# Two-layer hybrid attention kernel: joined head sums, shifted slots in heads and layer 1, another order at the passages to the out stages

## The reference

```python
for layer in range(2):
    shift, scale, gate = split(silu(c) @ ada_w[layer] + ada_b[layer], 3)
    h = rms_norm(x, norm_w[layer]) * (1 + scale) + shift
    y = even_mixer(h) if layer == 0 else odd_mixer(h)
    x = x + gate * y
return rms_norm(x, final_norm_w)
# even_mixer, 8 heads: q, k, v, z = h @ w_in
#   differential attention: (softmax(q0 k0) - lam * softmax(q1 k1)) @ v, rms_norm over 128, * silu(z)
#   gated delta rule: q, k = l2_normalize(silu(conv(.))); chunks of 64, triangular solve,
#   scan over the state, rms_norm over 128, * silu(z);      then @ w_out
# odd_mixer, 32 heads in 4 groups: sliding window attention (128) with sinks, * silu(z), @ w_out
```

## Time and profile before

| | us |
|---|---|
| median of three runs (2013.40 to 2019.76) | 2015.92 |
| the profiled execution | 2020.77 |
| its span, first to last instruction | 2019.0 |
| TensorE busy, 12628 matmul instructions | 1906.0 (94%) |
| DVE, ACT busy | 1140.4, 735.1 |
| start of one head's values to the next's | 121.2 |
[...]

### The profile page before, as it was taken

How to read it: one execution, slowest core, us unless ns; L and a number is a source line. 1 busy time by engine, 2 the same in 40 slices (tenths; PEclk the granted TensorE clock), 3 DMA queues, 4 the chain that set the end, 5 groups by cost and what they waited for, 6 DMA issues and landing times.

```text
span 2019.0 us, 30586 instructions
## 1 busy us (share of the span) xinstructions
PE 1906.0 (94%) x12628; PEld 1471.2 (73%) x12628; DVE 1140.4 (56%) x2147; ACT 735.1 (36%) x1548; POOL 6.4 (0%) x9
## 2 busy tenths in 40 slices
PE   6899999999999999999998799899999999998996
PEld 0367778777777877778776688777777777776885
DVE  2365665656656466655755656745665565563333
ACT  3352342424334242342524322634443443343221
POOL 0000000000000000000000000000000000000001
PEclk8999999999999999999998899999999999998998
DMA  9942322232322322322220777433223232313333
GB/s 393 408 162 101 119 101 95 102 118 94 127 94 95 126 84 107 121 97 95 109 101 1 261 241 234 149 131 125 99 94 131 96 114 109 126 53 110 120 114 115
DMA packets 58314, 266.29 MB, mean 132 GB/s; under 512 B 6465, under 2 KB 6849, under 8 KB 40641
## 3 DMA queue, kind: packets, MB, share of 16 engines
q1 hardware_dynamic: 58176, 264.35, 35.8%
HBM read 255.41 MB, written 8.91 MB: 131 GB/s over the span
## 4 chain that ended last, share of the span: by engine, by line
PE 77%; DVE 10%; ACT 6%; DMA 4%; issue 2%; SPq 0%; DVEq 0%; ACTq 0%
PE psum L554 22%; PE psum L555 20%; PE psum L556 20%; DMA ada_p<-in_ada_first 2%; PE psum L657 2%; PE psum L944 2%; ACT pr L1315 2%; DVE ada_acc L1403 1%; PE psum L956 1%; PE psum L972 1%; PE psum L799 1%; DVE pr L1822 1%; DVE pr L1838 1%; PE psum L567 1%; DVE pa L1666 1%
## 5 line engine op out<-in xcount | busy, mean ns | idle before, releaser
L554 PE MATMUL psum<-mov_hi,w_hi 128*128 128x512 f32 x2128 | 875.9, 412 | 35.3 <-DVE mov_lo L1738 11.3
L555 PE MATMUL psum<-mov_lo,w_hi 128*128 128x512 f32 x2128 | 837.4, 394 | 0.0
L556 PE MATMUL psum<-mov_hi,w_lo 128*128 128x512 f32 x2128 | 836.7, 393 | 0.0
L554 PEld LDWEIGHTS psum<-mov_hi,w_hi 128*128 128x128 f32 x2128 | 403.3, 190 | 156.5 <-issue 63.5
L556 PEld LDWEIGHTS psum<-mov_hi,w_lo 128*128 128x128 f32 x2128 | 403.6, 190 | 89.0
L1388 DVE TENSOR_TENSOR w_lo<-w_raw,w_hi 128x512 fp32r<-128x512 f32 x532 | 356.2, 686 | 195.3 <-ACT w_hi L1042 194.7
L555 PEld LDWEIGHTS psum<-mov_lo,w_hi 128*128 128x128 f32 x2128 | 404.4, 190 | 77.7 <-issue 3.8
L1042 ACT ACTIVATE w_hi<-w_raw 128x512 fp32r<-128x512 f32 x532 | 309.2, 621 | 1.9 <-DMA w_raw<-in_w_pack 1.4
L1403 DVE SCALAR_TENSOR_TENSOR ada_acc<-ada_t,silu_c,ada_acc 128x512 f32<-128x512 f32 x240 | 179.2, 747 | 5.7
L1315 ACT ACTIVATE pr<-pr,st 128x256 f32<-128x256 f32 x128 | 63.4, 498 | 114.6 <-DVE st L1831 114.6
L1272 ACT ACTIVATE osq<-res 128x512 f32<-128x512 f32 x30 | 19.0, 632 | 235.2 <-DVE res L1777 235.2
(11 more groups left out here) (279 smaller groups left out, 1621.9 us busy)
## 6 DMA issues: line engine op xcount, KB each, us to landing
w_raw<-in_w_pack SPq DMA_DIRECT2D x133, 1024.0 KB, 4.8
ada_t<-in_ada_late SPq DMA_DIRECT2D x128, 512.0 KB, 5.7
x_in<-in_ada_first SPq DMA_DIRECT2D x32, 512.0 KB, 9.3
ada_t<-in_ada_first SPq DMA_DIRECT2D x16, 512.0 KB, 9.1
ada_p<-in_ada_first SPq DMA_DIRECT2D x16, 512.0 KB, 9.6
res<-in_x_t SPq DMA_DIRECT2D x4, 1024.0 KB, 11.3
xr<-in_x_t SPq DMA_DIRECT2D x16, 256.0 KB, 3.7
x_spill<-res SPq DMA_DIRECT2D x16, 256.0 KB, 5.4
```

The source lines that it names most:

```text
L554: mm(PJ[r], w_hi[r][:, ks], mov_hi[:, kt], start=(j == 0), stop=False)
L555: mm(PJ[r], w_hi[r][:, ks], mov_lo[:, kt], start=False, stop=False)
L556: ins = mm(PJ[r], w_lo[r][:, ks], mov_hi[:, kt], start=False, stop=(j == KC - 1))
```

## The change

- Heads: combine(3) stands in DVE's slot 15 instead of 17 (DA_C).
- Heads: the four sums become four matmuls with 32 output columns each, placed side by side in TensorE's columns, into four 32-row bands of one bank (all_sums, slot 21). ACT takes one Ln and one Exp over all 128 rows, with a bias for each band, behind a preload of the table that has both. all_spread (slot 23) brings each band's row back to 128 rows by four matmuls with 32 input rows each. DVE reads two of the results in PSUM, ACT copies the other two (spread_copies).
- Out stage 0: the first two pairs of adaLN tiles are issued ahead of the wait for dy_ok.
- Layer 1: scores and what follows one slot later, second turns at 20, values at 25 (71 for w = 3), adaLN tiles in slots 2, 4, 5, 6 of each 16 instead of 1, 5, 9, 13, ada_stage in slot 59 instead of 64, v_group in 14 instead of 12.
- Passage to out stage 1: the first blocks of y are split in the last group's slots 62 and 63 (half_ok tells when TensorE has read those of mov_hi that they replace); turns in slots 65 and 66, values in 68; the first out chunk runs two slots ahead of the second (TAIL1), splits in the order SPLIT1.

```diff
...
     c["slope1"] = np.broadcast_to(2.0 ** (-8.0 * np.arange(1, 33) / 32), (P, 32))
+    c["part"] = np.broadcast_to(np.repeat([1.0, 1.0 / P], 32), (P, 64))
+    c["spread"] = np.broadcast_to(p[:, None] % 32 == 0, (P, P))
+    c["nbias"] = np.stack([np.repeat([4 * EPS, 4 * EPS, EPS, 0.0], 32), np.repeat([0.0, -0.5 * np.log(P), 0.0, 0.0], 32)], axis=1)
...
-        DA_S, DA_T = (0, 5, 8, 13), (5, 8, 13, 18)
+        DA_S, DA_C, DA_T = (0, 5, 8, 13), (4, 7, 12, 15), (5, 8, 13, 18)
...
+        L1_T = [[(16 * w + 17, 16 * w + 20) for w in range(4)] for g in range(NG1)]
+        L1_V = [[16 * w + 25 for w in range(3)] + [71] for g in range(NG1)]
+        L1_T[-1][3], L1_V[-1][3] = (65, 66), 68
+        TAIL1 = [((0, 0), (0, 1))] + [((1, n), (0, n + 2)) for n in range(5)] + [((1, 5),), ((1, 6),)]
+        SPLIT1 = [range(4, 8), range(8, 10), range(10, 12), range(12, 15), range(15, 16)]
+        L1_ADA = (2, 4, 5, 6)
...
-                    if not base:
+                    if not base and n > 0:
                         ada_pair(8 * B_OUT0 + 2 * n)
                         ada_pair(8 * B_OUT0 + 2 * n + 1)
...
             load_w(0, 2, N_OUT0 + 1)
+            for n in range(2):
+                ada_pair(8 * B_OUT0 + n)
             sp.wait_ge(dy_ok, NH0)
...
+                if done is not None:
+                    ins.then_inc(done, 1)
...
-            def norm_sums(h, i):
-                pe.wait_ge(sqn_ok, h * 2 + i + 1)
-                if i == 0:
-                    mm(SA0, ones, tmpK[:], start=True, stop=True).then_inc(ssn_ok, 1)
-                else:
-                    mm(SA1, ones, tmpQ[:], start=True, stop=True).then_inc(ssn_ok, 1)
+            def all_sums(before, h):
+
+                if h is not None:
+                    pe.wait_ge(sqn_ok, h * 2 + 2)
+                if before is not None:
+                    pe.wait_ge(gsq_ok, before + 1)
+                    pe.wait_ge(dsq_ok, before + 1)
+                for q, buf in enumerate((tmpK, tmpQ, tA, pa[1])):
+                    if (h, before)[q // 2] is not None:
+                        ins = mm(SA0[Q[q], :], con("part")[:, 32 * (q // 2):32 * (q // 2) + 32], buf[:], start=True, stop=True,
+                                 tile_position=(0, 32 * q))
+                ins.then_inc(sums_ok, 1)
+
+            def all_spread(before, h):
+
+                pe.wait_ge(rn_ok, (before + 1 if h is None else h) + 1)
+                if before is not None:
+                    pe.wait_ge(ATev_ok, before * 4 + 4)
+                    pe.wait_ge(vn_ok, before * 4 + 4)
+                for q, out in enumerate((SA0, SA1, TR, GW)):
+                    if (h, before)[q // 2] is not None:
+                        ins = mm(out, con("spread", Q[q]), tmpK[Q[q], :], start=True, stop=True, tile_position=(32 * q, 0))
+                ins.then_inc(spread_ok, 1)
 
             def g_rows(h):
 
...
+                st[21] = [lambda: all_sums(before, h)]
+                st[23] = [lambda: all_spread(before, h)]
...
-                    st.setdefault(16 * w + 8, []).append(lambda w=w: scores1(g, w, 0))
-                    st.setdefault(16 * w + 10, []).append(lambda w=w: scores1(g, w, 1))
-                    st.setdefault(16 * w + 16, []).append(lambda w=w: turn1(g, 2 * w))
-                    st.setdefault(16 * w + 19, []).append(lambda w=w: turn1(g, 2 * w + 1))
-                    st.setdefault(16 * w + 22, []).append(lambda w=w: values1(g, w))
-                st[64].append(lambda: ada_stage(B_L1 + g, GW))
+                    st.setdefault(L1_T[g][w][0], []).append(lambda w=w: turn1(g, 2 * w))
+                    st.setdefault(L1_T[g][w][1], []).append(lambda w=w: turn1(g, 2 * w + 1))
+                    st.setdefault(L1_V[g][w], []).append(lambda w=w: values1(g, w))
+                    st.setdefault(16 * w + 9, []).append(lambda w=w: scores1(g, w, 0))
+                    st.setdefault(16 * w + 11, []).append(lambda w=w: scores1(g, w, 1))
+                st[59].append(lambda: ada_stage(B_L1 + g, GW))
...
+                    proj_slot(N_L1 + c, 8, g, s % SLOTS, free, done=half_ok if g == NG1 - 1 and s == 8 * SLOTS - 5 else None)
...
-                for c in range(2 if s < SLOTS - 1 else 0):
-                    proj_slot(N_OUT1 + c, 0, 0, s, ((q1_ok, z1_ok)[c], 4 * NG1), first=3 * KC)
+                for c, part in TAIL1[s]:
+                    proj_slot(N_OUT1 + c, 0, 0, part, ((q1_ok, z1_ok)[c], 4 * NG1), first=3 * KC)
...
             def all_rstd(before, h):
 
-
-
-                if before is not None:
-                    act.wait_ge(gss_ok, before + 1)
-                    step(f(tA[:], TR, ACT.Ln, scale=1.0 / P, bias=EPS))
-                    act.wait_ge(dss_ok, before + 1)
-                    step(f(pa[1][:], GW, ACT.Ln, scale=1.0 / P, bias=small[:, LEPS:LEPS + 1]))
-                if h is not None:
-                    for i, (dst, src) in enumerate(((tmpK, SA0), (tmpQ, SA1))):
-                        act.wait_ge(ssn_ok, h * 2 + i + 1)
-                        step(f(dst[:], src, ACT.Ln, bias=4 * EPS))
-                    for i, dst in enumerate((tmpK, tmpQ)):
-                        f(dst[:], dst[:], ACT.Exp, scale=-0.5, bias=(0.0, -0.5 * float(np.log(P)))[i]).then_inc(rn_ok, 1)
-                if before is not None:
-                    f(pa[1][:], pa[1][:], ACT.Exp, scale=-0.5).then_inc(drn_ok, 1)
-                    f(tA[:], tA[:], ACT.Exp, scale=-0.5).then_inc(grn_ok, 1)
+                rows = slice(0 if h is not None else 64, P if before is not None else 64)
+                nc.scalar.preload_act_table_set("natural_log_exp_and_others")
+                act.wait_ge(sums_ok, (before + 1 if h is None else h) + 1)
+                step(f(tmpK[rows, :], SA0[rows, :], ACT.Ln, bias=small[rows, NBIAS:NBIAS + 1]))
+                f(tmpK[rows, :], tmpK[rows, :], ACT.Exp, scale=-0.5, bias=con("nbias", rows)[:, 1:2]).then_inc(rn_ok, 1)
+
+            def spread_copies(before, idx):
+
+                act.wait_ge(spread_ok, idx + 1)
+                f(pa[1][:], GW, ACT.Copy).then_inc(drn_ok, 1)
+                f(tA[:], TR, ACT.Copy).then_inc(grn_ok, 1)
 
             def tail_stages(h):
...
                 st = head_stages(h)
...
-                    st.setdefault(16 * w + 16, []).append(lambda w=w: turn1_copy(g, 2 * w))
-                    st.setdefault(16 * w + 19, []).append(lambda w=w: turn1_copy(g, 2 * w + 1))
+                    st.setdefault(16 * w + 12, []).append(lambda w=w: exps1(g, 2 * w))
+                    st.setdefault(16 * w + 14, []).append(lambda w=w: exps1(g, 2 * w + 1))
+                    st.setdefault(L1_T[g][w][0], []).append(lambda w=w: turn1_copy(g, 2 * w))
+                    st.setdefault(L1_T[g][w][1], []).append(lambda w=w: turn1_copy(g, 2 * w + 1))
                 return st
 
...
                         h()
                     if s % 2 == 0:
                         split_hi(N_L1 + s // SLOTS + 1, 8, g, s % SLOTS // 2)
+                if g == NG1 - 1:
+                    split_y1(range(2, 4))
                 z1_tanh(g, 3)
+
+            def split_y1(ks):
+
+                for k in ks:
+                    act.wait_ge(y1_ok, k + 1)
+                    f(mov_hi[:, k * T:k * T + T], res[:, k * T:k * T + T], ACT.Copy).then_inc(hi_ok, 1)
 
             group(0)
             for g in range(1, NG1):
                 group(g, g - 1)
             tail = merged({}, group_stages(NG1 - 1))
-            for s in range(SLOTS):
+            for s in range(len(SPLIT1)):
                 for h in tail.get(s, []):
                     h()
-                for k in (2 * s, 2 * s + 1):
-                    act.wait_ge(y1_ok, k + 1)
-                    f(mov_hi[:, k * T:k * T + T], res[:, k * T:k * T + T], ACT.Copy).then_inc(hi_ok, 1)
-                if s < 4:
-                    split_hi(N_OUT1 + 1, 0, 0, s)
+                split_y1(SPLIT1[s][:2])
+                for q in ((0, 1), (2,), (3,), (), ())[s]:
+                    split_hi(N_OUT1 + 1, 0, 0, q)
+                split_y1(SPLIT1[s][2:])
 
             def final_scale(i, c):
...
                 V.tensor_copy(tile4(gB[:]), head_col(gate_g, h).to_broadcast([P, 4, P])).then_inc(gB_ok, 1)
 
             def norm_mul(h):
-                for i, (dst, n) in enumerate(((ck, tmpK), (cq, tmpQ))):
-                    dve.wait_ge(rn_ok, h * 2 + i + 1)
-                    V.tensor_tensor(dst[:], dst[:], n[:], ALU.mult).then_inc(qkn_ok, 1)
+                dve.wait_ge(spread_ok, h + 1)
+                for dst, n in ((ck, SA0), (cq, SA1)):
+                    V.tensor_tensor(dst[:], dst[:], n, ALU.mult).then_inc(qkn_ok, 1)
 
             def decay_exponents(h):
 
...
-                    st.setdefault(DA_T[b] - 1, []).append(lambda b=b: combine(h, b))
+                    st.setdefault(DA_C[b], []).append(lambda b=b: combine(h, b))
                 st.setdefault(24, []).append(lambda: gated(h, GO, tA, WDN, NH0, grn_ok, gy_ok))
...
             def group_stages(g):
```

(43 more changed lines are left out.)

36 lines of the change are left out of this document (16 added, 20 removed).

## The result

| | before | after |
|---|---|---|
| median (lowest to highest) of four runs, us | 2015.68 (2013.40 to 2019.76) | 1962.41 (1960.63 to 1966.31) |
| profiled execution, us | 2020.77 | 1966.31 |
| its span, us | 2019.0 | 1964.5 |
| mean granted TensorE clock | 0.979 | 0.981 |

In the traces the granted clock stands at 1.00 or at 0.50: in before it is 1.00 over 366.0 to 373.0, 0.50 over 373.2 to 376.4 and 1.00 over 376.6 to 383.0. At 1.00 split matmuls start 0.23 us apart, with records of 0.39 us; at 0.50 (before, from 1846.33 on) it is 0.43 us, with records of 0.63 us: a record outlasts the distance to the next start. One call of an unsplit float32 matmul left two instructions (L762, L805). A stretch with both levels has their mean, as 0.83 in the earlier trace rows.

What follows compares the result with a forecast made beforehand. TensorE, busy nearly the whole span, was taken to bound the kernel through its waits. Heads 25.6, out stage 0 3.0, layer 1 11.2, out stage 1 10.0, start -0.3: 49.5 us off 2015.9 gives 1966.4, range 1950 to 1986.

Steps and rivals of the forecast that it cites:

- The turn's wait: Heads, fourth turn: TensorE's 2.04 us idle goes in seven heads with combine(3) earlier, 14.3 us.
- the wait moves: Rival, heads: TensorE waits instead for the squares at slot 21 or rn_ok at slot 23; 1981 us, chance 0.14.
- The clock: Heads: a gain of 5.1 us in the granted TensorE clock.
- Joined sums and gate rows: Heads: tiled sums and spreads save 0.8 us a head, 5.6 us in seven; gate rows' waits go, 1.5 us.
- The second table load: Heads, ACT: the load moves to z_tanh in slot 32, its 1.28 us covered; uncovered, up to 10 us lost.
- Passage to out stage 0: After the last head: adaLN pairs issued earlier bring the weights earlier, less the tail's longer chain; net 3.0 us.
- I charge 0.3 us: Last head's tail: cost of the exposed chain of sums, Ln, Exp, spread and copies, 0.3 us.
- Layer 1's groups: Layer 1: scores a slot later let a projection slot cover q1_copy, removing waits of 9.0 + 2.2 = 11.2 us.
- the turns' 5.5 us stay: Layer 1: the waits ahead of the turns, 5.5 us, remain, so zero gain there.
- Passage to out stage 1: Layer 1's end: third out chunk at t + 31.4, before 39.64 us after t, the last group's slot 64; 10.0 us gained.
- the weights need what they needed: Passage to out stage 1: from the gating to the third chunk still 11.0 us, so 20.4 + 11.0 = t + 31.4.
- Start: Kernel's start: constants grow by 0.1 MB ahead of TensorE's first work, -0.3 us; head 0 pays 0.9 us for its sums.

Runs made afterwards that it cites:

- combine alone: The kernel before with combine(3) in DVE's slot 15 and nothing else of the change: 1997.97 us, ratio 0.9904 to before.
- combine back: The kernel after with combine(3) back in DVE's slot 17, all else kept: 1983.45 us, ratio 0.9824 to before.
- pairs held: The kernel after, SyncE holding out stage 0's third and fourth adaLN pairs until ACT begins splitting the third chunk's weights: 1965.1 us, ratio 0.9740.
- Weights first: The kernel after, ACT splitting the third chunk's weights ahead of its wait for the first chunk's result at out stage 1's passage: 1963.43 us, ratio 0.9730.

## Why the prediction was right, and where it was off

- **The turn's wait, right.** 14.3 us for seven heads. Seven times 2.24 us is what the traces give, 15.7 us; the forecast counted the idle alone. The margin was as walked: combine(3) ends at 250.0, 1.25 us ahead of the turn at 251.27, for 1.24 forecast. The rival that the wait moves is out.
- **The clock, right:** 5.1 us forecast. No run shows this term as it stands; what combine alone and combine back show in its place is 4.7 and 4.4 us, for three stretches of 3.4 us each whose granted clock goes from 0.50 to 1.00.
- **Joined sums and gate rows, under-sized.** 0.8 us a head and 0.2 for the gate rows; measured 1.43, of which 0.95 and 0.45 are placed. The step that failed most is the gate rows' "1.5 us gained", which counts 0.21 us of idle a head where the stall cost 0.45. In the groups themselves two errors offset each other, which is luck: "1.12 us for each four" is 0.86, since four run wholly side by side, and "0.1 us on entering and on leaving" is 0.33 and 0.41 us a group. That gives 1.19 and 1.27 us for 1.32 each. ACT's chain was as walked: one load ahead of the sums, Ln, Exp, the copies 1.2 us behind the spread's start:

```profile
257.19 1.28 ACT L1207 ACT_TABLE_LOAD   x1
259.31 0.69 ACT L1209 ACTIVATE tmpK<-psum,small 128x512 f32<-128x512 f32 x1 [0.84 <-PE psum L639]
260.03 0.72 ACT L1210 ACTIVATE tmpK<-tmpK,const 128x512 f32<-128x512 f32 x1
...
263.33 0.60 ACT L1215 ACTIVATE pa<-psum 128x512 f32<-128x512 f32 x1 [2.05 <-PE psum L651]
```

- **The second table load, right.** At 276.70, in a gap of ACT of 4.85 us and 0.96 us ahead of what tanh waits for:

```profile
276.70 1.28 ACT L1146 ACT_TABLE_LOAD   x1 [4.85 <-DVE qg L1595]
278.94 0.60 ACT L1146 ACTIVATE cq<-psum 128x512 f32<-128x512 f32 x1 [0.96 <-PE psum L567]
```

- **Passage to out stage 0, over-sized:** 3.0 us forecast, 0.2 in this trace, some 1.6 over several. Two steps failed. "I take 3.3 us" set the pairs' share of the transfer at over 2 us; pairs held puts two pairs at 0.1 to 1.0, and I overlooked that the next two pairs would follow sooner. And "I charge 0.3 us" for the tail's chain is a term that no run shows: at a granted clock of 1.00 the chain took 9.34 us, for 9.37 in before, and at 0.50 it took 11.08, 1.7 us more. The forecast counts nothing for such a stretch.
- **Layer 1's groups, under-sized:** 11.2 forecast, 16.7 measured. The waits ahead of the scores went as said. The step that failed is "9.0 + 2.2 = 11.2 us": it counts the idle alone, and a stall costs more than its idle (0.38 us by the blocks above, some 5 us in all). And that the turns' 5.5 us stay was 1.3 us off: 4.2 are left. Waits went in the blocks w = 3, which I had not seen; that ada_stage's 0.79 us now stand ahead of those turns fits, and no run here puts it behind them.
- **Passage to out stage 1: 10.0 forecast, 8.9 measured.** The early part was right to a tenth: first out chunk at t + 3.8 (t = 1759.93), values at t + 18.6, and the last gating at t + 20.4 (1780.36), the 20.4 that the sum takes; it is shown by this run alone. The step that failed is "the weights need what they needed": the third chunk came at t + 33.8, not 31.4. I took the wait of before, which ended with the transfer, to be the transfer still, and didn't ask what else would stand in ACT's queue. Weights first gives 2.1 of these 2.4 us back. The 10.0 us as a whole is shown by no run; the traces show 6.5 us up to the third chunk and 2.4 behind it. There the granted clock is 1.00 in after (1793.7 to 1846.0), where before has 0.50 over 1844.4 to 1851.0.
- **Start: -1.2 us forecast** for head 0 and the constants, beside 2.2 gained by head 1's turn; together 0.5 came out, so 1.7 were lost. The traces of the other kernels have values of head 1 at 251.8 to 253.1 with the same program up to there, so against the 251.4 us that before has without the turn's wait the price is 0.5 to 1.7 us. Combine alone, which pays none of it, has 252.0, so that part of this may be scatter of the start; the price by itself stays open.

## What to carry to other kernels

Count a removed stall at its idle plus what the stream behind it loses (0.2 to 0.4 us here), and a stall of 2 us at up to 1.6 us of clock more. When a wait is removed, list every later item in the queue of the engine that releases it, not only the one whose record ended it: a transfer that ended the wait before isn't what ends it next. A form that is cheaper under cover (joined sums) can be dearer in a tail, where each of its hops is exposed and the granted clock can be 0.50 (the spread took 2.07 us there, for 1.07 in head 1); keep both forms.
